# Two transformer blocks on one core: the seven-product block scheme of the first gated MLP begins one pair of loads later, with token sums read from PSUM and gate rows kept there

## Chip, cores, metric

One core of one Trainium2 chip. Times are device microseconds of one execution. The kernel before was timed in three runs.

## What is computed

Two blocks of a transformer, 512 tokens, width 1024. Each is a mixer (projections, attention or pooling, output projection), a norm with the residual, and a gated MLP with its norm. The change is inside the first block's MLP:

```python
h = rms_norm(x, ln_pre_ffn[l])
f = (jax.nn.silu(h @ w_gate[l]) * (h @ w_up[l])) @ w_down[l]
x = x + rms_norm(f, ln_post_ffn[l])
```

`w_gate` and `w_up` are 1024 x 2816, `w_down` is 2816 x 1024. All is float32.

## The kernel before

**Numbers in two parts.** Each operand of a product is split in a high part and the rest: ScalarE writes `hi` (a copy rounded to the TensorE format), VectorE (in the mixers also GpSimd) writes `lo` = raw - hi. TensorE forms hi x hi, hi x lo and lo x hi: three products for each one wanted (`products`, L1951 to L1957, whose three lines are L1954 to L1956).

**Gate and up.** `h`, turned so that features lie on partitions, is in `h_hi` and `h_lo` (8 feature groups x 512 tokens). The weights come in loads of 256 columns, gate and up in turn, 11 pairs, into the two slots of `w_raw`. A load is split by quarters (`split_hi` L1073, `split_lo` L1455).

The first pair is *straight* (`up_products` L2204): each load gives two outputs of 128 columns, in PSUM banks 0 to 3. It is formed in halves of 256 tokens, since the second half of the tokens still comes out of the norm meanwhile. A method `pair` for further straight pairs, with products of 512 tokens, is there; only the second layer runs it (ten pairs).

The other ten pairs are 20 *blocks*, `N_BLOCK = N_UP - 2` (L647), one for each load. A block is a 2 x 2 arrangement (128 columns x half of the features, half of the features x 256 tokens), formed with seven half-size products instead of eight. It needs:

- sums of its weights: GpSimd, `block_sums` L980, four operations of 128x512 into `w_sum`, written to S1, S2, S4, S3;
- sums of the tokens, once for all blocks: `t_sums`, four of 128x1024, split into `t_hi`, `t_lo` (the fourth over the free parts of `h_hi`, `h_lo`). VectorE makes sums 1, 2 and 4 (L1750 to L1769, L1738), GpSimd sum 3 (`third_turned_sum` L1008), each from high and low parts;
- the seven weight pieces S1, A11, A12, S4, S2, S3, A22, each split by ScalarE (`hi` L1262, line L1263) and VectorE (`lo` L1728, line L1730).

A *part* (L2245) is one such half-size product: 4 feature groups x 3, so 12 instructions of 256 tokens. It waits until its piece's low part is done. Blocks are interleaved (`block_period` L2255): S2 of this block, S1 and A11 of the next, S3 of this one, A12 and S4 of the next, A22 of this one. The accumulators are banks 4, 5, 6 for even blocks (gate) and 0, 1, 2 for odd ones (up): `acc(name, e)` L675. Two parts wait for sums that VectorE forms out of the accumulators (`sum_done`).

**Gate times up.** VectorE forms three sums for each block out of an accumulator and a copy that ScalarE made (`p1`, `p35`, `p5`), in lines L1788, L1808 and L1826, and reads the fourth quarter straight from bank A. For a gate block the sums go to `act_gate` in SBUF, and ScalarE applies SiLU there in place (L1333, L1344, and L1354 from PSUM). For an up block they go to `hid`, which is then multiplied by `act_gate` (L1833 for one row of 512 tokens, L1840 and L1845 for the halves of the other).

**What sets the order.** Each engine runs a program written out by hand, in order, with semaphores between: `begin` (L1271 ScalarE, L1750 VectorE) for the first blocks, `period` (L1312, L1785) for each block after that. SyncE issues the loads (`blocks` L780), each when its slot's pieces are split.

**Around it.** Ahead stands the norm: VectorE scales a token tile (`h_tok`, L1494), TensorE turns it (L1966) into PSUM (tiles 2 and 3 into banks 4 to 7), ScalarE copies the high part and VectorE the low part (L1499). Behind stand the down projection (`row_products` L2176, lines L2168 to L2172), token tile t into banks 2t and 2t+1. In its first load the last two parts of the last block (`last_p7`, `last_p4`) are put between the tiles.

## Time and profile before

| | us |
|---|---|
| median of three runs | 1368.21 (1367.76 to 1371.12) |
| profiled execution, its own time | 1370.78 |
| its span, first to last instruction | 1369.0 |
| TensorE busy in it | 1310.7 (96%) |
| VectorE | 819.0 (60%) |
| ScalarE | 665.8 (49%) |
| GpSimd | 487.0 (36%) |
| mean granted TensorE clock | 0.99 |

Times in the trace count from the first instruction. The MLP's gate and up products run from 236.8 to 485; the blocks begin at 266.65. An engine is busy while it works on an instruction; matmuls overlap, so the rate is read from the distance between starts, not from the length of one. In brackets behind a row stands how long the engine was idle before it and which line ended that.

### The profile page before, as it was taken

The numbers are of one execution on the slowest core, as the hardware profiler recorded it, in microseconds if no ns is written. First come the engines' busy times: TensorE is split into PE (matmuls) and PEld (weight loads), VectorE is DVE, ScalarE is ACT, GpSimd is POOL, SyncE is SP. The second block draws the span as 40 slices with busy tenths as digits, with TensorE's granted clock in tenths as the row PEclk, the third lists the DMA queues.
The fourth block names the chain that finished last, engine by engine and source line by source line (L and its number), as shares of the span: only waits on it lengthen the run. The fifth ranks groups of instructions, "written<-read, shape, count | busy, mean of one in ns | idle before, by whom it ended". The sixth has DMA issues, their size and how long they took to land.

```text
span 1369.0 us, 21443 instructions
## 1 busy us (share of the span) xinstructions
PE 1310.7 (96%) x7576; PEld 1167.2 (85%) x7576; DVE 819.0 (60%) x1507; ACT 665.8 (49%) x1310; POOL 487.0 (36%) x580
## 2 busy tenths in 40 slices
PE   8999989889999999999999997899999999999998
PEld 7999867889999988878999887779888888888877
DVE  4676736999999833363566665435655555533454
ACT  4666735445555522245667675524433434322352
POOL 5554682765656300046757766611000000000000
PEclk9999999999999999999999999999999999999999
DMA  6222213133233332222212322222233222222221
GB/s 185 65 66 78 63 72 113 34 121 123 92 105 109 114 102 92 85 67 73 70 47 62 71 62 77 93 96 78 93 114 99 93 92 92 92 94 96 87 92 62
DMA packets 120502, 120.52 MB, mean 88 GB/s; under 512 B 22604, under 2 KB 107291, under 8 KB 120434
## 3 DMA queue, kind: packets, MB, share of 16 engines
q1 hardware_dynamic: 118336, 112.92, 26.6%
q0 software_dynamic: 2096, 6.71, 1.5%
q8 instruction: 40, 0.66, 0.2%
q14 instruction: 28, 0.23, 0.1%
q10 hardware_dynamic: 2, 0.00, 0.0%
HBM read 117.52 MB, written 2.10 MB: 87 GB/s over the span
## 4 chain that ended last, share of the span: by engine, by line
PE 43%; DVE 4%; POOL 4%; ACT 3%; issue 2%; POOLq 0%; DVEq 0%; ACTq 0%
PE ps L1954 7%; PE ps L1956 7%; PE ps L1955 7%; PE ps L2168 4%; PE ps L2172 4%; PE ps L2170 4%; PE ps L2047 2%; PE ps L2040 2%; PE ps L2042 2%; ACT ring L1156 1%; POOL qk_rs L865 1%; POOL w_lo L903 1%; DVE ring L1579 1%; DVE prob L1622 1%; PE ps L2132 1%
## 5 line engine op out<-in xcount | busy, mean ns | idle before, releaser
L1954 PE MATMUL ps<-h_hi,w_hi 128*128 128x256 f32 (+1 forms) x784 | 259.9, 332 | 0.2 <-DVE w_lo L1459 0.2
L1956 PE MATMUL ps<-h_hi,w_lo 128*128 128x256 f32 (+1 forms) x784 | 258.4, 330 | 0.0
L1955 PE MATMUL ps<-h_lo,w_hi 128*128 128x256 f32 (+1 forms) x784 | 258.3, 329 | 0.0
L1459 DVE TENSOR_TENSOR w_lo<-w_raw,w_hi 128x512 fp32r<-128x512 f32 x220 | 140.0, 689 | 148.6 <-ACT w_hi L1082 148.6
L1082 ACT ACTIVATE w_hi<-w_raw 128x512 fp32r<-128x512 f32 x220 | 122.9, 620 | 181.6 <-PE ps L2172 163.4
L2168 PE MATMUL ps<-w_hi,st_hi 128*128 128x512 f32 x432 | 171.8, 398 | 2.7 <-DVE st_lo L1706 1.9
L2172 PE MATMUL ps<-w_hi,st_lo 128*128 128x512 f32 x432 | 171.1, 396 | 0.0
L2170 PE MATMUL ps<-w_lo,st_hi 128*128 128x512 f32 x432 | 171.1, 396 | 0.0
L2040 PE MATMUL ps<-w_hi,h_hi 128*128 128x384 f32 (+2 forms) x528 | 168.7, 329 | 2.3 <-DVE work L1561 2.0
L2042 PE MATMUL ps<-w_hi,h_lo 128*128 128x384 f32 (+2 forms) x528 | 164.8, 322 | 0.0
L1954 PEld LDWEIGHTS ps<-h_hi,w_hi 128*128 128x128 f32 x784 | 149.9, 191 | 14.2 <-DVE w_lo L1459 0.4
L1955 PEld LDWEIGHTS ps<-h_lo,w_hi 128*128 128x128 f32 x784 | 149.9, 191 | 13.1
L1956 PEld LDWEIGHTS ps<-h_hi,w_lo 128*128 128x128 f32 x784 | 149.7, 191 | 13.3
L864 POOL TENSOR_SCALAR x_ss<-x_ss 128x1 f32<-128x1 f32 x20 | 10.6, 531 | 394.8 <-ACT junk L1102 394.1
L903 POOL TENSOR_TENSOR w_lo<-w_raw,w_hi 128x384 fp32r<-128x384 f32 (+2 forms) x146 | 142.1, 988 | 21.6 <-ACT w_hi L1094 18.7
L2047 PE MATMUL ps<-w_lo,h_hi 128*128 128x384 f32 (+2 forms) x528 | 108.8, 325 | 5.7 <-POOL w_lo L903 4.9
L1173 ACT ACTIVATE prob<-prob,neg_max 128x512 f32<-128x512 f32 (+3 forms) x128 | 72.1, 563 | 82.5 <-DVE neg_max L1622 82.1
L2040 PEld LDWEIGHTS ps<-w_hi,h_hi 128*128 128x128 f32 x528 | 100.4, 190 | 4.1 <-DVE work L1561 2.2
L937 POOL TENSOR_TENSOR prob<-prob,rden 128x512 f32<-128x512 f32 (+1 forms) x96 | 69.1, 720 | 94.1 <-DVE rden L1682 93.7
L2042 PEld LDWEIGHTS ps<-w_hi,h_lo 128*128 128x128 f32 x528 | 100.7, 191 | 1.1
L2168 PEld LDWEIGHTS ps<-w_hi,st_hi 128*128 128x128 f32 x432 | 81.8, 189 | 21.9 <-issue 2.3
L2172 PEld LDWEIGHTS ps<-w_hi,st_lo 128*128 128x128 f32 x432 | 81.8, 189 | 19.1
(248 smaller groups left out, 2749.8 us busy)
## 6 DMA issues: line engine op xcount, KB each, us to landing
w_raw<-in_w_up_dram SPq DMA_DIRECT2D x33, 1024.0 KB, 5.1
w_raw<-in_w_down_dram SPq DMA_DIRECT2D x22, 1024.0 KB, 4.9
w_raw<-in_w_in_dram SPq DMA_DIRECT2D x72, 256.0 KB, 3.5
w_raw<-in_w_gate_dram SPq DMA_DIRECT2D x11, 1024.0 KB, 5.3
w_raw<-in_w_out_dram SPq DMA_DIRECT2D x8, 1024.0 KB, 5.0
w_raw<-in_w_in_dram SPq DMA_DIRECT2D x32, 128.0 KB, 2.7
w_raw<-in_w_ple_gate_dram SPq DMA_DIRECT2D x4, 1024.0 KB, 5.1
x<-in_x_dram SPq DMA_DIRECT2D x4, 512.0 KB, 5.6
```

What stands on the lines that cost most here:

```text
L903: pool.tensor_tensor(w_lo[:, c % 2, q], w_raw[:, c % 2, q], w_hi[:, c % 2, q].bitcast(F32), ALU.subtract)\
L1082: act.activation(w_hi[:, slot, q], w_raw[:, slot, q], ACT.Copy).then_inc(hi_done, 1)
L1459: dve.tensor_tensor(w_lo[:, slot, q], w_raw[:, slot, q], w_hi[:, slot, q].bitcast(F32), ALU.subtract).then_inc(lo_done, 1)
L1954: pe.matmul(out_, s_hi, m_hi, start=first and n == 0, stop=False, skip_group_check=True)
L1955: pe.matmul(out_, s_hi, m_lo, start=False, stop=False, skip_group_check=True)
L1956: mm = pe.matmul(out_, s_lo, m_hi, start=False, stop=last and n == len(pairs) - 1, skip_group_check=True)
L2040: pe.matmul(bank, h_hi[:, kb0 + i, tok], hi[:, i, :], start=half == 0 and i == 0, stop=False, skip_group_check=True)
L2042: pe.matmul(bank, h_lo[:, kb0 + i, tok], hi[:, i, :], start=False, stop=False, skip_group_check=True)
L2047: mm = pe.matmul(bank, h_hi[:, kb0 + i, tok], lo[:, i, :], start=False, stop=half == 1 and i == KH - 1, skip_group_check=True)
L2168: pe.matmul(bank, rows_hi[:, k, tok], hi[:, k, col], start=first and k == 0, stop=False, skip_group_check=True)
L2170: pe.matmul(bank, rows_hi[:, k, tok], lo[:, k, col], start=False, stop=False, skip_group_check=True)
L2172: mm = pe.matmul(bank, rows_lo[:, k, tok], hi[:, k, col], start=False, stop=last and k == RB - 1, skip_group_check=True)
```

## The change

- Straight pairs are now two. `up_products` runs `pair(1)` after the halves, and `N_BLOCK` is 18. The chunk numbers behind it move by two, so each slot keeps its parity. ScalarE and VectorE split the two additional loads in `begin`, VectorE multiplies two more rows (`first_pairs`), and the loads of the blocks start at column 512.
- Token sums: all four on VectorE (`token_sum`), GpSimd's is gone. Where the second half of the tokens is wanted, it is read from the turned tiles that still lie unsplit in banks 4 to 7 (`unsplit`), so a sum is one or two operations instead of two or three.
- For even blocks the sums of the gate go to bank 7 (`gate_row`, 512 tokens) and to half of bank 3 (`late_gate`); SiLU works there in place and the multiplications read it there. The last quarter (`early_gate`) stays in SBUF.
- The down projection begins with tile 2, then 3, 1, 0, with a wait for the last reading of bank 7 before tile 3 and of bank 3 before tile 1 (`late_gate_read`).

```diff
-        N_BLOCK = N_UP - 2
+        N_BLOCK = N_UP - 4
...
+        gate_row = ps[:, 7, :]
+        late_gate = ps[:, 3, TOK2]
+        early_gate = act_gate[:, 1, TOK1]
+        def unsplit(half):
+            return ps[:, 4 + half:8:2, :].rearrange("p t (k n) -> p t k n", n=P)
...
                 for e, w in enumerate((gate, up)):
-                    sp.wait_ge(lo_done, 4 * (C_UP1 + e + 1))
-                    sp.dma_start(by_cols((C_UP1 + e) % 2)[0], cols(w, CW)).then_inc(raw_block[e], 16)
+                    sp.wait_ge(lo_done, 4 * (C_UP1 + e + 3))
+                    sp.dma_start(by_cols((C_UP1 + e) % 2)[0], cols(w, 2 * CW)).then_inc(raw_block[e], 16)
...
             block_sums(0, 0, first=True)
-            third_turned_sum()
             block_sums(1, 1, first=True)
...
 ScalarE, begin:
+                    for m in range(2):
+                        act.wait_ge(products_done, G_UP1 + m + 1)
+                        act.activation(act_gate[:, m, :], ps[:, m, :], ACT.Silu).then_inc(gate_silu, 1)
+                    for q in range(4):
+                        split_hi(C_UP1 + 2, C_UP1 % 2, q, G_UP1 + 2)
                     act.wait_ge(t_sum, 1)
                     turned_hi(1)
+                    for q in range(4):
+                        split_hi(C_UP1 + 3, (C_UP1 + 1) % 2, q, G_UP1 + 4)
+                    act.wait_ge(t_sum, 2)
+                    turned_hi(2)
+                    act.wait_ge(t_sum, 3)
+                    turned_hi(3)
+                    for m in range(2):
+                        act.wait_ge(products_done, G_UP1 + m + 5)
+                        act.wait_ge(hid_done, m + 1)
+                        act.activation(act_gate[:, m, :], ps[:, m, :], ACT.Silu).then_inc(gate_silu, 1)
...
-                        act.activation(act_gate[:, 0, :], act_gate[:, 0, :], ACT.Silu).then_inc(gate_silu, 1)
+                        act.activation(gate_row, gate_row, ACT.Silu).then_inc(gate_silu, 1)
...
-                        act.activation(act_gate[:, 1, TOK2], act_gate[:, 1, TOK2], ACT.Silu)
+                        act.activation(late_gate, late_gate, ACT.Silu)
...
 VectorE, begin:
+                    token_sum(1)
+                    for q in range(4):
+                        split_lo(C_UP1 + 2, C_UP1 % 2, q)
+                    token_sum(2)
+                    first_pairs(0, 0)
+                    first_pairs(0, 1)
+                    token_sum(3)
+                    for q in range(4):
+                        split_lo(C_UP1 + 3, (C_UP1 + 1) % 2, q)
+                    for n in range(3):
+                        turned_lo(n + 1)
+                    token_sum(4)
                     for n, name in enumerate(("S1", "A11", "A12", "S4")):
                         lo(name, 0, n + 1)
+                    first_pairs(1, 0)
+                    first_pairs(1, 1)
                     lo("A22", 0, 5)
                     lo("S2", 0, 6)
+                    lo("S1", 1, 7)
                     dve.wait_ge(part_done, 3)
                     dve.wait_ge(part_copied, copies_made(0, 2))
-                    dve.tensor_tensor(act_gate[:, 0, TOK1], p1[:, 0, :], acc("C", 0), ALU.add).then_inc(sum_done, 1)
+                    dve.tensor_tensor(gate_row[:, TOK1], p1[:, 0, :], acc("C", 0), ALU.add).then_inc(sum_done, 1)
                     lo("A11", 1, 8)
                     lo("S3", 0, 9)
                     lo("A12", 1, 10)
                     lo("S4", 1, 11)
                     lo("A22", 1, 12)
...
+                def token_sum(n):
+                    dst = by_tiles(t_sums[n - 1][:, :, :])
+                    if n == 2:
+                        dve.wait_ge(t_sum, 1)
+                        dve.tensor_tensor(dst, unsplit(1), by_tiles(t_sums[0][:, :, :]), ALU.subtract).then_inc(t_sum, 1)
+                        return
+                    if n == 4:
+                        dve.wait_ge(t_sum, 2)
+                        hi, lo = (tokens_of(h, 1, TOK1).bitcast(F32) for h in (h_hi, h_lo))
+                        link(dve.tensor_tensor(t_sums[3][:, :, :], hi, t_sums[1][:, :, :], ALU.subtract))
+                        dve.tensor_tensor(t_sums[3][:, :, :], t_sums[3][:, :, :], lo, ALU.add).then_inc(t_sum, 1)
+                        return
+                    hi, lo = (tokens_of(h, 0, (TOK1, TOK2)[n // 2]).bitcast(F32) for h in (h_hi, h_lo))
+                    link(dve.tensor_tensor(dst, unsplit(n // 2), by_tiles(hi), ALU.subtract))
+                    dve.tensor_tensor(t_sums[n - 1][:, :, :], t_sums[n - 1][:, :, :], lo, ALU.subtract).then_inc(t_sum, 1)
+                def first_pairs(i, m):
+                    dve.wait_ge(gate_silu, 2 * i + m + 1)
+                    dve.wait_ge(products_done, G_UP1 + 4 * i + m + 3)
+                    dve.tensor_tensor(hid[:, 2 * i + m, :], act_gate[:, m, :], ps[:, 2 + m, :], ALU.mult).then_inc(hid_done, 1)
...
 VectorE, period:
-                    dve.tensor_tensor(row, row, act_gate[:, 0, :], ALU.mult).then_inc(hid_done, 1)
+                    dve.tensor_tensor(row, row, gate_row, ALU.mult).then_inc(hid_done, 1)
...
-                    dve.tensor_tensor(row, row, act_gate[:, 1, TOK2], ALU.mult)
+                    return dve.tensor_tensor(row, row, late_gate, ALU.mult)
...
 TensorE:
                 if b == 1:
+                    pair(1)
                     return
...
-            row_products(N_DOWN, C_DOWN1, N_OUT, 2, order=(3, 2, 1, 0), bank_waits={2: [(gate_silu, MT)], 0: [(hid_done, MT)]},
-                         between={2: last_p7, 1: last_p4})
+            row_products(N_DOWN, C_DOWN1, N_OUT, 2, order=(2, 3, 1, 0),
+                         bank_waits={2: [(gate_silu, MT)], 3: [(hid_done, MT - 1)], 1: [(late_gate_read, 1)],
+                                     0: [(hid_done, MT)]}, between={3: last_p7, 1: last_p4})
```

## Rows read from the trace of the kernel before

**Rows 1.** Stretches: busy us of PE, PEld, DVE, ACT, POOL; clock; DMA; GB/s.
```profile
264.00:294.00 30.00, 21.30 (x140) 20.80 (x139) 28.47 (x31) 13.98 (x27) 17.61 (x11) 0.83 0.33 106
294.00:334.00 40.00, 40.00 (x337) 39.94 (x336) 36.16 (x46) 22.96 (x46) 22.68 (x16) 1.00 0.33 106
```

**Rows 2.** Waits of TensorE, 264 to 293.4: total us, times, longest.
```profile
PE ps L1954 <- DVE w_lo L1730: 4.5, 2, 2.5
PE ps L1954 <- DVE act_gate L1788: 4.2, 1, 4.2
```

**Rows 3.** Timeline of TensorE (start, us, instruction): ends of the stretch.
```profile
263.87 0.28 PE L1956 MATMUL ps<-h_hi,w_lo 128*128 128x256 f32 x1
...
476.49 0.39 PE L2168 MATMUL ps<-w_hi,st_hi 128*128 128x512 f32 x1
```

**Rows 4.** Timeline of TensorE, steady blocks.
```profile
293.40 0.28 PE L1954 MATMUL ps<-t_hi,w_hi 128*128 128x256 f32 x1
...
303.42 0.28 PE L1954 MATMUL ps<-t_hi,w_hi 128*128 128x256 f32 x1
...
387.05 0.38 PE L1954 MATMUL ps<-h_hi,w_hi 128*128 128x256 f32 x1
...
465.05 0.28 PE L1954 MATMUL ps<-t_hi,w_hi 128*128 128x256 f32 x1
```

**Rows 5.** TensorE, second layer: groups of 955 to 1250, timeline rows.
```profile
L1954 PE MATMUL ps<-h_hi,w_hi 128*128 128x512 f32 x320 | 124.5, 389 | 0.0
...
963.18 0.40 PE L1954 MATMUL ps<-h_hi,w_hi 128*128 128x512 f32 x1
...
1180.81 0.40 PE L2168 MATMUL ps<-w_hi,st_hi 128*128 128x512 f32 x1
```

**Rows 6.** Timeline of ScalarE: a SiLU at the start and the last one.
```profile
255.54 0.60 ACT L1273 ACTIVATE act_gate<-ps 128x512 f32<-128x512 f32 x1 [3.43 <-PE ps L1956]
...
475.26 0.38 ACT L1354 ACTIVATE act_gate<-ps 128x256 f32<-128x256 f32 x1 [0.54 <-PE ps L1956]
```

**Rows 7.** Timeline of VectorE at the start, then its steady low pieces grouped.
```profile
244.59 1.27 DVE L1494 SCALAR_TENSOR_TENSOR h_tok<-x,x_rs,gain_pre 128x1024 f32<-128x1024 f32 x1
246.32 2.28 DVE L1494 SCALAR_TENSOR_TENSOR h_tok<-x,x_rs,gain_pre 128x1024 f32<-128x1024 f32 x1 [0.46 <-POOL x_rs L865]
...
253.49 3.31 DVE L1755 TENSOR_TENSOR t_sum<-t_sum,h_lo 128x1024 f32<-128x1024 f32 x1
...
264.68 1.22 DVE L1736 TENSOR_TENSOR t_lo<-t_sum,t_hi 128x1024 fp32r<-128x1024 f32 x1
265.82 0.68 DVE L1730 TENSOR_TENSOR w_lo<-w_sum,w_hi 128x512 fp32r<-128x512 f32 x1
...
281.34 2.52 DVE L1730 TENSOR_TENSOR w_lo<-w_sum,w_hi 128x512 fp32r<-128x512 f32 x1
...
L1730 DVE TENSOR_TENSOR w_lo<-w_sum,w_hi 128x512 fp32r<-128x512 f32 x71 | 68.0, 967 | 7.7 <-ACT w_hi L1263 7.5
```

**Rows 8.** Timeline of GpSimd: two weight sums.
```profile
246.26 1.26 POOL L993 TENSOR_TENSOR w_sum<-w_raw 128x512 f32<-128x512 f32 x1
...
390.29 1.63 POOL L1003 TENSOR_TENSOR w_sum<-w_raw,w_sum 128x512 f32<-128x512 f32 x1
```

**Rows 9.** DMA issues of 225 to 300: KB each, median us to landing.
```profile
w_raw<-in_w_gate_dram SPq DMA_DIRECT2D x3, 1024.0 KB, 5.2
```

**Rows 10.** Timeline of VectorE in steady blocks: sums and gated products.
```profile
386.50 0.41 DVE L1845 TENSOR_TENSOR hid<-ps,act_gate 128x256 f32 x1
...
390.68 0.41 DVE L1826 TENSOR_TENSOR act_gate<-ps,p 128x256 f32<-128x256 f32 x1
...
399.56 1.78 DVE L1833 TENSOR_TENSOR hid<-hid,act_gate 128x512 f32 x1
...
403.13 1.40 DVE L1840 TENSOR_TENSOR hid<-hid,act_gate 128x256 f32 x1
```

**Rows 11.** Timeline of TensorE: the last token tile of the norm.
```profile
248.66 1.09 PE L1966 MATMUL ps<-ident,h_tok 128*128 128x128 f32 x8 [1.65 <-DVE h_tok L1494]
```

More of the change, by code:

```diff
@@ L619, in two_blocks_kernel @@
         part_copied = sem("part_copied")
+        late_gate_read = sem("late_gate_read")
         t_sum = sem("t_sum")
-        t3_sum = sem("t3_sum")
         t_hi_done = sem("t_hi_done")
@@ L681, in raw_blocks, with by_tiles @@
             return 8 * j + (16 - 8 * e)
+        gate_row = ps[:, 7, :]
[3 more added lines that the diff above has]
+            return ps[:, 4 + half:8:2, :].rearrange("p t (k n) -> p t k n", n=P)
+        def by_tiles(rows):
+            return rows.rearrange("p k (t n) -> p t k n", n=P)
         def hid_row(n, tok):
@@ L780, in blocks @@
             def blocks(gate, up):
+                for i in range(2):
+                    for e, w in enumerate((gate, up)):
+                        load(C_UP1 + 2 * i + e, (C_UP1 + e) % 2, cols(w, CW * i))
                 for e, w in enumerate((gate, up)):
-                    load(C_UP1 + e, (C_UP1 + e) % 2, cols(w, 0))
-                for e, w in enumerate((gate, up)):
-                    sp.wait_ge(lo_done, 4 * (C_UP1 + e + 1))
-                    sp.dma_start(by_cols((C_UP1 + e) % 2)[0], cols(w, CW)).then_inc(raw_block[e], 16)
+                    sp.wait_ge(lo_done, 4 * (C_UP1 + e + 3))
+                    sp.dma_start(by_cols((C_UP1 + e) % 2)[0], cols(w, 2 * CW)).then_inc(raw_block[e], 16)
                 with sp.Fori(1, N_BLOCK // 2) as i:
@@ L1284, in begin @@
                     hi("S4", 0)
-                    act.wait_ge(t_sum, 2)
-                    turned_hi(2)
-                    act.wait_ge(products_done, G_UP1 + 4)
+                    act.wait_ge(products_done, G_UP1 + 8)
                     hi("A22", 0)
                     hi("S2", 0)
+                    act.wait_ge(t_sum, 4)
+                    turned_hi(4)
                     act.wait_ge(part_done, 1)
@@ L1353, in period @@
                     if e == 0:
-                        act.activation(act_gate[:, 1, TOK1], acc("A", e), ACT.Silu).then_inc(gate_silu, 1)
+                        act.activation(early_gate, acc("A", e), ACT.Silu).then_inc(gate_silu, 1)
                     if not last:
@@ L1736, in turned_lo @@
                     dve.tensor_tensor(low, t_sums[n - 1][:, :, :], hi.bitcast(F32), ALU.subtract).then_inc(t_lo_done, 1)
-                def difference(n, half, tok, other):
-                    dst = t_sums[n - 1][:, :, :]
-                    link(dve.tensor_tensor(dst, tokens_of(h_hi, half, tok).bitcast(F32), t_sums[other - 1][:, :, :],
-                                           ALU.subtract))
-                    dve.tensor_tensor(dst, dst, tokens_of(h_lo, half, tok).bitcast(F32), ALU.add).then_inc(t_sum, 1)
@@ L1745, in first_pair @@
-                def first_pair(m):
-                    dve.wait_ge(gate_silu, m + 1)
-                    dve.wait_ge(products_done, G_UP1 + m + 3)
-                    dve.tensor_tensor(hid[:, m, :], act_gate[:, m, :], ps[:, 2 + m, :], ALU.mult).then_inc(hid_done, 1)
+                def token_sum(n):
[13 more added lines that the diff above has]
+                    dve.tensor_tensor(t_sums[n - 1][:, :, :], t_sums[n - 1][:, :, :], lo, ALU.subtract).then_inc(t_sum, 1)
@@ L1755, in begin @@
-                    link(dve.tensor_tensor(t1, t1, tokens_of(h_lo, 0, TOK2).bitcast(F32), ALU.add))
-                    dve.tensor_tensor(t1, t1, tokens_of(h_lo, 0, TOK1).bitcast(F32), ALU.subtract).then_inc(t_sum, 1)
-                    dve.wait_ge(t_sum, 1)
-                    difference(2, 1, TOK2, 1)
-                    turned_lo(1)
+                    token_sum(1)
+                    for q in range(4):
+                        split_lo(C_UP1 + 2, C_UP1 % 2, q)
+                    token_sum(2)
@@ L1781, in sums_to @@
                 def sums_to(p, e, m, tok):
-                    return act_gate[:, m, tok] if e == 0 else hid_row(p + (m + 1), tok)
+                    return (late_gate if m else gate_row[:, tok]) if e == 0 else hid_row(p + (m + 3), tok)
                 def period(p, e, last=False, low_turned=None):
@@ L1856, in block_swiglu @@
                 dve.wait_ge(part_copied, copies_made(p, 3))
-                dve.tensor_tensor(hid_row(p + 1, TOK2), acc("A", 1), p35[:, 1, :], ALU.add).then_inc(sum_done, 1)
+                dve.tensor_tensor(hid_row(p + 3, TOK2), acc("A", 1), p35[:, 1, :], ALU.add).then_inc(sum_done, 1)
                 gated(p)
                 dve.wait_ge(part_done, parts_done(p, 2))
-                dve.tensor_tensor(hid_row(p + 2, TOK2), acc("A", 1), p5[:, 1, :], ALU.add).then_inc(sum_done, 1)
-                late_gated(p)
+                dve.tensor_tensor(hid_row(p + 4, TOK2), acc("A", 1), p5[:, 1, :], ALU.add).then_inc(sum_done, 1)
+                late_gated(p).then_inc(late_gate_read, 1)
                 dve.wait_ge(part_done, parts_done(p, 3))
-                dve.tensor_tensor(hid_row(p + 2, TOK1), acc("A", 1), act_gate[:, 1, TOK1], ALU.mult).then_inc(hid_done, 1)
+                dve.tensor_tensor(hid_row(p + 4, TOK1), acc("A", 1), early_gate, ALU.mult).then_inc(hid_done, 1)
             def conv_swiglu(c0, g0, st0):
```

50 lines of the change are left out of this document (12 added, 38 removed).

## Prediction

> **What bounds the kernel now.** I read the busy time by stage first. In the steady part of the gate and up products TensorE has no idle time. In the first 30 us of the block products it is busy for 21.3, at a mean granted clock of 0.83 [rows 1]. The waits of that stretch name the cause: 4.5 us for low weight pieces (`w_lo` L1730) and 4.2 us for one sum (`act_gate` L1788), all from VectorE [rows 2], which is itself busy for 28.5 of the 30 us [rows 1]. So the stage is bound by TensorE, except at its start, where VectorE's queue decides.
>
> The size of it: the last product of the straight pair issues at 263.87, so the next could at 263.99; the first row product of the down projection issues at 476.49 [rows 3]. Between them lie 138 parts of 12 products: 19 whole blocks of seven, and five parts. A block without a wait takes 303.42 - 293.40 = 10.02 us, so a part takes 1.431 us [rows 4]. 138 parts are 197.5 us, and the stretch is 212.5: 15.0 us are lost. From 303.42 to 465.05 lie 16 blocks in 161.63 us, against 160.3: 1.3 us, in small gaps once in two blocks, such as the one before the product at 387.05 [rows 4]. The other 13.7 are lost at the start: 8.7 as waits, about 5 at the lower clock and around the restarts [rows 1 to 3].
>
> **The change part by part.** Times below are those of before, unshifted, unless said.
>
> *One pair of loads straight, 18 blocks for 20.* A straight pair is 96 products of 512 columns. The second layer's ten such pairs, 320 products on each of three lines, take 1180.81 - 963.18 = 217.6 us, so a pair is 21.8 us [rows 5]. Two blocks are 20.0. The new stretch is 21.8 + 124 x 1.431 = 199.2 us, against 212.5. If nothing at all is lost, 13.3 us are saved. The arithmetic alone costs 1.8; the rest is what the straight pair covers. What the start loses afterwards must be taken off.
>
> *Does the straight pair start without a wait?* It needs its gate chunk split. ScalarE does the second SiLU after the second gate product, about 258.5 (the first began at 255.54 [rows 6]), then four quarters of the same 512 elements as that SiLU, 0.60 each [rows 6]: 261.5. VectorE takes 0.68 a quarter when alone [rows 7] and follows to about 262.2, before 264.0. On VectorE this split stands behind token sum 1, which is now two operations where it was three, and none of the slow ones at 3.31 us [rows 7], since GpSimd has nothing to do then. Alone, 1024 elements take 1.2 us [rows 7]: it ends at about 254.5. The up chunk is needed 48 products later, at 274.9. VectorE gets there after token sum 2, two `hid` rows and token sum 3, at 267.3; alone its quarters end at 270.0, and with one weight sum of GpSimd (1.26 us [rows 8]) before each of them at 275.1. I take 273.7 and no wait, with 0.2 us as the bad end.
>
> *Are the first blocks ready at 285.8?* GpSimd's weight sums wait for a load now issued behind the gate chunk's low split at 262.2, landing 5.2 us later [rows 9], and run from 267.5 to about 275. ScalarE's high pieces of block 0 follow at 275.5 to 278. VectorE: up chunk to 273.7, then GpSimd's last sum to 275, three low token sums and token sum 4 (five operations of 1.2) to 281, and four pieces, one sum of GpSimd among them, to 285. The first is there at 281.7, four us before its part, and each of the others too. The token operations that stood between the pieces before are gone or done.
>
> *The wait that is added.* `first_pairs(1, 1)` stands on VectorE before pieces A22, S2 and S1 of the next block, and waits for the last product of the straight pair, at 285.8. Behind it are queued a `hid` row, eight low pieces and two sums, wanted one by one: the fifth part at 291.5, the eighth (S3, with its sum) at 295.8. Counted to that sum: 0.68 + 8 pieces + 2 x 0.41 [rows 7, 10]. At 0.68 a piece that is 6.9 us; at the steady mean of 0.967 [rows 7] it is 9.2; there are 10.0. So it fits with little room. I take 0.8 us for the start, and keep 0 and 9.0 (below) as ends.
>
> *The weight sums leave the stretch 246 to 267.* The first of them began at 246.26 [rows 8], and the scaling of the last token tile beside it took 2.28 us [rows 7] where its neighbour of the same size took 1.27 [rows 7]. TensorE waited 1.65 us for it at 248.66 [rows 11]. Without the sum it ends 1.0 earlier. ScalarE's and VectorE's copies of the tile (1.0 and 1.2) then still end before TensorE's next 24 products do, so 1.0 us is saved. The low end is 0, if another wait ends last there.
>
> *Gate rows in two PSUM banks.* Per two blocks, three sums write PSUM, two SiLU go PSUM to PSUM, and two multiplications read one operand there. The multiplications took 1.78 and 1.40 us because both inputs lay in SBUF and GpSimd was at work [rows 10]. A sum with one input from PSUM took 0.41 at 390.68 although GpSimd's sum ran from 390.29 to 391.92 [rows 8, 10]. So I expect 0.7 and 0.4, some 2.1 us of VectorE per pair. That by itself is off the path. But the gap before 387.05 ends just after the multiplication of L1845 (386.50 to 386.91 [rows 10]), which stands behind them in the queue; 0.7 us earlier removes it. Of 8 pairs x 0.16 = 1.3 us I leave 0.4. No row shows a write to PSUM by either engine here. From the nearest rows, sums of 0.41 and SiLU of 0.60, its cost lies between -0.1 and +0.3 us an operation. The five on VectorE then add 1.5 us a pair at most, less than the 2.1 it gets back.
>
> The Trainium skill (SBUF — State Buffer, Who interferes with whom) says that VectorE with two SBUF inputs and GpSimd exclude each other while they read, and that with one SBUF input it does not. By that rule the two multiplications lose their stretch entirely, and the trace agrees (1.78 against 0.41). Against the change speaks the table in VectorE: DVE Perf Modes, The TRN2 errata, which gives an operation from PSUM 62 cycles more than one from SBUF; by it, as an estimate, 65 ns are added to each of five operations a pair, 3 us of VectorE time in all, and the sum would stay, as VectorE does not bound there. The trace does not agree: its SBUF rows of 512 and 1024 elements, 0.68 and 1.22, put 256 elements at 0.41, and the row with a PSUM input has 0.41.
>
> *The end of the stage.* The down projection now begins with tile 2, whose bank is read by the last SiLU. That ran 475.26 to 475.64, and the row product came at 476.49 [rows 3, 6]: 0.85 us to spare. Tile 3 waits for a multiplication of bank 7 that has a row tile and a part, 4.2 us, to get done; `late_gate_read` has longer. Nothing.
>
> **The sum.** 13.3 + 1.0 - 0.8 - 0.4 = 13.1, rounded down to 13.0 us. The profiled execution took 1370.78 us with a span of 1369.0, so its like would take 1357.8. It was 2.6 above the median of 1368.21, from which I take the forecast: **1355.2 us**.
>
> **The rivals.**
> 1. *The queue behind the held `hid` row is late.* It takes the place of the waits removed. If the eight pieces take 1.78 us each, as the multiplication of the same size did beside GpSimd [rows 10], VectorE needs 15.7 us for 10.0: TensorE waits 5.7, and a wait like that costs some 3.3 in clock afterwards (5 were lost around 8.7). 13.3 + 1.0 - 9.0 - 0.4 gives 4.9: 1363.3. For it: such durations are frequent at the start before. Against: each needs a GpSimd sum at its side, and only four to six fall in these 10 us. The mild half, 1 to 5 us lost, is likelier than the full price.
> 2. *Only the straight pair does anything:* reads of PSUM don't free VectorE and the token tile wins nothing. The gaps stay at 1.3 and the 1.0 is not had: 13.3 - 0.8 - 1.3 = 11.2, so 1357.0. The 0.41 beside a running GpSimd speaks against it.
> 3. *Slower.* The same place as rival 1, at the price of the longest piece of the old start, 2.5 us (281.34 [rows 7]): 8 x 2.52 + 1.5 = 21.7, TensorE waits 11.7, and with the clock 15.0. Then 13.3 + 1.0 - 15.0 - 0.4 = -1.1: 1369.3. It decides from 13.9 us lost, a piece mean of about 2.4. It goes over 0.3% slower when the up chunk of the straight pair is late by 3 us too: 1372.5. GpSimd has about eight sums of 1.3 us in the whole start, too few for that.
>
> **How the numbers follow.** Forecast 0.66 (1353.5 to 1358 by itself, with the run to run spread of 1367.8 to 1371.1 in mind), rival 1 0.18, mostly below 1361, rival 2 0.07, rival 3 0.09 with its neighbours, of which 0.04 is slower by over 0.3% and 0.05 no difference. A measurement of this kernel can tell 0.3%, 4.1 us, from no change. The range reaches to the middle of rival 1: 1353.2 to 1361.0. Faster 0.91, within 0.3% 0.05, slower 0.04.
>
> **What would show it.** Right: between the two straight pairs TensorE does not idle; the second takes 21.8 us; the block products begin with waits under 1 us in sum, and the granted clock stays at 1.00 from 236 on; `hid` multiplications take 0.7 and 0.4; the wait for the last token tile shrinks to about 0.65; the first row product of the down projection comes 13 us sooner. Wrong: TensorE waits for `w_lo` L1730 or for a sum in `ps` after the second pair, and the clock falls there; or a part of each block waits for `sum_done`, 18 times over. The forecast falls above all if VectorE, after its hold, is not back in step by the eighth part.

## The result and the profile after

Six runs of the changed kernel have a median of 1357.88 us (1357.60 to 1358.93), six of the kernel before 1369.80 (1367.76 to 1372.36). The ratio is 0.9914, with a 95% interval of 0.9901 to 0.9926: 11.9 us faster. The forecast was 1355.2, with a range to 1361.0. Its base of 1368.21, the median of three runs, turned out 1.6 below that of six, and its gain of 13.0 is 1.1 more than was had.

| | before | after |
|---|---|---|
| span of the profiled execution | 1369.0 | 1356.3 |
| TensorE busy | 1310.7 | 1305.6 |
| VectorE | 819.0 | 799.5 |
| ScalarE | 665.8 | 659.8 |
| GpSimd | 487.0 | 465.3 |

First the stretches, which answer to [rows 1]. The columns are the same.

```profile
236.00:264.00 28.00, 27.15 (x214) 26.12 (x213) 20.42 (x23) 14.98 (x23) 8.13 (x10) 1.00 0.24 75
264.00:286.00 22.00, 22.00 (x103) 18.35 (x102) 20.39 (x19) 7.47 (x12) 8.39 (x5) 1.00 0.30 96
286.00:296.00 10.00, 10.00 (x83) 9.88 (x82) 7.70 (x10) 7.32 (x14) 5.72 (x6) 1.00 0.34 107
296.00:306.00 10.00, 7.40 (x61) 7.03 (x60) 10.00 (x11) 4.66 (x11) 7.63 (x5) 1.00 0.66 210
306.00:346.00 40.00, 40.00 (x338) 40.00 (x337) 37.36 (x47) 22.96 (x47) 23.78 (x17) 1.00 0.34 106
```

TensorE is busy without a gap from 264 to 296, where before it had 21.30 of 30 us. It loses 2.6 us between 296 and 306, and there VectorE is busy for 10.00 of 10. The granted clock is 1.00 (2.4 GHz) in every row; in [rows 1] it was 0.83. The waits of TensorE from 230 to 312 (total, times, longest), for [rows 2]:

```profile
PE ps L1984 <- DVE h_tok L1503: 1.8, 2, 1.1
PE ps L1972 <- DVE ps L1806: 1.4, 1, 1.4
PE ps L1972 <- issue: 1.2, 1, 1.2
PE ps L1972 <- DVE w_lo L1468: 0.2, 1, 0.2
```

Of the first row, 0.66 us is the wait for the last token tile (1.65 in [rows 11]). Where 4.5 us of low pieces and 4.2 us of a sum stood, there is one wait of 1.4 us for a sum, and one of 1.2 for which the view names no engine. The timeline of TensorE gives their places and the marks used below; it answers to [rows 3, 4, 11]:

```profile
238.69 0.28 PE L1972 MATMUL ps<-h_hi,w_hi 128*128 128x256 f32 x1
...
249.54 1.09 PE L1984 MATMUL ps<-ident,h_tok 128*128 128x128 f32 x8 [0.66 <-DVE h_tok L1503]
...
264.87 0.40 PE L1972 MATMUL ps<-h_hi,w_hi 128*128 128x512 f32 x1
...
286.65 0.28 PE L1972 MATMUL ps<-t_hi,w_hi 128*128 128x256 f32 x1
...
298.22 0.39 PE L1972 MATMUL ps<-t_hi,w_hi 128*128 128x256 f32 x1 [1.37 <-DVE ps L1806]
...
303.99 0.36 PE L1972 MATMUL ps<-h_hi,w_hi 128*128 128x256 f32 x1 [1.23 <-issue]
...
305.49 0.28 PE L1972 MATMUL ps<-t_hi,w_hi 128*128 128x256 f32 x1
...
455.79 0.28 PE L1972 MATMUL ps<-t_hi,w_hi 128*128 128x256 f32 x1
...
467.24 0.39 PE L2186 MATMUL ps<-w_hi,st_hi 128*128 128x512 f32 x1
```

The second straight pair runs from 264.87 to 286.65, 21.78 us, with no wait before it. The blocks then run to the first row product at 467.24. Their 124 parts at 1.431 would take 177.5 us and took 180.59, so 3.1 are lost. All of it is lost at the start: from 305.49 to 455.79 lie 15 blocks in 150.30 us, 10.02 each.

The timeline of VectorE shows why, and what came before:

```profile
248.20 1.29 DVE L1503 SCALAR_TENSOR_TENSOR h_tok<-x,x_rs,gain_pre 128x1024 f32<-128x1024 f32 x1 [0.47 <-POOL x_rs L877]
...
260.45 2.50 DVE L1468 TENSOR_TENSOR w_lo<-w_raw,w_hi 128x512 fp32r<-128x512 f32 x4 [4.98 <-ACT w_hi L1084]
...
268.13 4.69 DVE L1468 TENSOR_TENSOR w_lo<-w_raw,w_hi 128x512 fp32r<-128x512 f32 x4
...
280.73 0.69 DVE L1739 TENSOR_TENSOR w_lo<-w_sum,w_hi 128x512 fp32r<-128x512 f32 x1
...
286.92 0.69 DVE L1767 TENSOR_TENSOR hid<-act_gate,ps 128x512 f32<-128x512 f32 x1 [2.01 <-PE ps L1974]
...
289.77 0.97 DVE L1739 TENSOR_TENSOR w_lo<-w_sum,w_hi 128x512 fp32r<-128x512 f32 x1 [0.96 <-ACT w_hi L1265]
291.17 0.43 DVE L1792 TENSOR_TENSOR ps<-p,ps 128x256 f32<-128x256 f32 x1 [0.42 <-PE ps L1974]
...
293.60 1.76 DVE L1739 TENSOR_TENSOR w_lo<-w_sum,w_hi 128x512 fp32r<-128x512 f32 x1
295.29 2.53 DVE L1739 TENSOR_TENSOR w_lo<-w_raw,w_hi 128x512 fp32r<-128x512 f32 x1
297.74 0.42 DVE L1806 TENSOR_TENSOR ps<-ps,p 128x256 f32<-128x256 f32 x1
...
302.68 1.21 DVE L1745 TENSOR_TENSOR h_lo<-t_sum,h_hi 128x1024 fp32r<-128x1024 f32 x1
```

The straight chunks are split in time: the gate chunk by 262.95 for 264.87, the up chunk by 272.82 for a product some 11 us after 264.87. The first piece of a block is there at 281.4. Then the `hid` row of the straight pair holds VectorE until 286.92. From there to the end of the sum in L1806, at 298.16, it takes 11.2 us: two waits of 0.96 and 0.42, and two pieces of 1.76 and 2.53. TensorE goes on 0.06 us after that sum. The second wait ends at 303.99, 0.10 us after the operation of L1745, which is `turned_lo(4)`, the low part of the fourth token sum. So the "issue" of the waits view is a wait for VectorE too; the kernel below in which `turned_lo(4)` stands earlier has no such wait.

**Marks.** In what follows, *stretch* is the time from the first gate product (238.69 here) to the first row product of the down projection (467.24): 228.55 us. Before, it ran from 236.83 to 476.49 [rows 3]: 239.66. The difference is 11.1. The trace's own clock shows the row product only 9.25 us sooner, since this execution reached its first gate product 1.86 later.

### The profile page after: what moved, and what is told of

It is laid out like the page before. It is cut to its first block, busy times and chain, and to the rows that moved or that the text cites. A ratio compares the mean times of both kernels' runs of the same rounds, so it can differ in the third digit from the quotient of the medians.

```text
span 1356.3 us, 21161 instructions
## 1 busy us (share of the span) xinstructions
PE 1305.6 (96%) x7504; PEld 1159.7 (86%) x7504; DVE 799.5 (59%) x1494; ACT 659.8 (49%) x1297; POOL 465.3 (34%) x569
## 4 chain that ended last, share of the span: by engine, by line
PE 43%; DVE 4%; POOL 4%; ACT 3%; issue 2%; POOLq 0%; DVEq 0%; ACTq 0%
PE ps L1972 7%; PE ps L1973 7%; PE ps L1974 7%; PE ps L2186 4%; PE ps L2188 4%; PE ps L2190 4%; PE ps L2058 2%; PE ps L2065 2%; PE ps L2060 2%; ACT ring L1158 1%; POOL qk_rs L877 1%; POOL w_lo L915 1%; DVE ring L1588 1%; DVE prob L1631 1%; PE ps L2150 1%
## 5 line engine op out<-in xcount | busy, mean ns | idle before, releaser
L1468 DVE TENSOR_TENSOR w_lo<-w_raw,w_hi 128x512 fp32r<-128x512 f32 x228 | 147.1, 698 | 155.2 <-ACT w_hi L1084 155.2
L1084 ACT ACTIVATE w_hi<-w_raw 128x512 fp32r<-128x512 f32 x228 | 127.3, 621 | 185.1 <-PE ps L2190 164.7
```

The source lines that it names most:

```text
L1084: act.activation(w_hi[:, slot, q], w_raw[:, slot, q], ACT.Copy).then_inc(hi_done, 1)
L1468: dve.tensor_tensor(w_lo[:, slot, q], w_raw[:, slot, q], w_hi[:, slot, q].bitcast(F32), ALU.subtract).then_inc(lo_done, 1)
```

## The experiments

Each was profiled once; those with an interval were also timed against the kernel before, whose medians beside them were 1368.43 to 1370.02. The last column is the time of the blocks, from their first part to the first row product.

| kernel | us | ratio to before | stretch | blocks |
|---|---|---|---|---|
| before | 1369.80 | | 239.66 | 209.84 |
| the kernel before, again | 1370.21 (one) | | 239.45 | 209.61 |
| after | 1357.88 | 0.9914 (0.9901 to 0.9926) | 228.55 | 180.59 |
| after, again | 1358.89 | 0.9921 (0.9905 to 0.9938) | 228.54 | 180.59 |
| after, token sums as before | 1357.10 | 0.9911 (0.9895 to 0.9928) | 229.41 | 180.57 |
| after, gate rows in SBUF | 1361.25 | 0.9942 (0.9925 to 0.9958) | 229.90 | 181.96 |
| after, straight pair alone | 1360.04 (one) | | 230.76 | 181.94 |
| before, gate rows in PSUM | 1368.03 | 0.9991 (0.9981 to 1.0001) | 238.38 | 208.55 |
| after, GpSimd beside the last tile | 1359.50 (one) | | 229.53 | 180.57 |
| after, other order at the start | 1357.53 | 0.9917 (0.9901 to 0.9933) | 227.38 | 179.44 |
| other order at the start, second form | 1357.64 | 0.9915 (0.9900 to 0.9931) | 227.40 | 179.45 |
| after, small weight sums | 1356.86 (one) | | 226.85 | 178.89 |
| blocks at once | 1362.19 | 0.9951 (0.9936 to 0.9965) | 230.61 | 203.46 |

**The yardstick: both kernels again.** No edit in either.

> The changed kernel a second time, for a second trace. From the first product of the gate and up stage to the first row product of the down projection the first trace took 228.6 us (before: 239.7). If that stretch is what the change moved and the rest of the span is execution to execution variation, it is 228.6 within 0.3 again, while the parts outside it may move by one or two us. If the 1.9 us that the stage began later belongs to the change, it begins at 238.7 again, against 236.8 before.

> The kernel before a second time, for a second trace. If the start of the stage and the time after it vary between executions of one kernel, its first gate product comes at another time than 236.8 by a us or more, or the span behind the first row product of the down projection differs from 892.5 by one to three us; the stretch between them stays at 239.7 within 0.3. If the change moved them, both stay as they were.

The stretch came out at 228.54 and 239.45, within 0.01 and 0.21 of the first profiles. The change is worth 11.0 us in it (10.9 and 11.1); the 11.9 of the medians, with its interval of 10.1 to 13.6, holds that. The rest of the program does not repeat so well: the first gate product comes between 236.6 and 239.2 in these profiles, and the time from the first row product to the second layer's first 512-column product lies between 483.1 and 486.7, in either kernel. The later begin in the first profile of the changed kernel is not the change's doing either, as the second profile of the kernel before has it at 239.06. So terms of about 1 us are read from the stretch and not from medians.

**Token sums as before, all else of the change kept.**

```diff
+                    if n == 1:
+                        t1 = t_sums[0][:, :, :]
+                        link(dve.tensor_tensor(t1, tokens_of(h_hi, 0, TOK2).bitcast(F32), tokens_of(h_hi, 0, TOK1).bitcast(F32), ALU.subtract))
+                        link(dve.tensor_tensor(t1, t1, tokens_of(h_lo, 0, TOK2).bitcast(F32), ALU.add))
+                        dve.tensor_tensor(t1, t1, tokens_of(h_lo, 0, TOK1).bitcast(F32), ALU.subtract).then_inc(t_sum, 1)
+                        return
...
+            third_turned_sum()
```

> The changed kernel with the token sums formed as before: three operations for the first on VectorE, two for the second, the third on GpSimd directly after the norm, all from high and low parts in SBUF. Theory (the straight pair makes the room, the PSUM reads only add to it): VectorE loses 1.2 + 3 x 2.1 us beside GpSimd before the gate chunk's low split, which then ends about 264 to 265 and delays the second straight pair by 0 to 1.5 us; the up chunk and the blocks aren't later, since VectorE has slack of 2 us before 286.8; start losses stay at 3.1. Sum: 0 to 2 us slower than the changed kernel, 1358 to 1360. Rival (without the PSUM reads the start is as late as before): TensorE waits 5 us or more between the two pairs or at the first block, 1363 or more.

The timeline of VectorE in this kernel, at token sum 1 and the split of the gate chunk:

```profile
254.71 3.31 DVE L1762 TENSOR_TENSOR t_sum<-t_sum,h_lo 128x1024 f32<-128x1024 f32 x1
258.05 3.32 DVE L1763 TENSOR_TENSOR t_sum<-t_sum,h_lo 128x1024 f32<-128x1024 f32 x1
261.29 4.71 DVE L1475 TENSOR_TENSOR w_lo<-w_raw,w_hi 128x512 fp32r<-128x512 f32 x4
```

With GpSimd's third sum back at their side, the operations take 3.31 again, as in [rows 7], and the gate chunk is split only by 266.00. The second straight pair waits 0.57 us for it, and the blocks start 0.88 us later in the stretch. From there on nothing differs (180.57 against 180.59). So reading the turned tiles from PSUM and taking the third sum from GpSimd, which were not tried one by one, are together worth 0.86 us, by letting the straight pair start in time. The medians do not resolve it: this kernel's, 1357.10, lies 0.8 and 1.8 below the two of the changed kernel, where it was expected up to 2 above.

**Gate rows in SBUF, all else of the change kept.**

```diff
-        gate_row = ps[:, 7, :]
-        late_gate = ps[:, 3, TOK2]
+        gate_row = act_gate[:, 0, :]
+        late_gate = act_gate[:, 1, TOK2]
...
                     dve.wait_ge(part_copied, copies_made(0, 2))
+                    dve.wait_ge(hid_done, 3)
```

The added wait keeps the first sum from overwriting the straight pair's gate row before it is read.

> The changed kernel with the gate rows in SBUF as before (gate_row and late_gate in act_gate), all else as changed. Theory: the gated multiplications take 1.78 and 1.40 us again instead of 0.7 and 0.4, and the gaps of 0.1 to 0.2 us before every second block's first h product return: 15 blocks of the steady part take 1.0 to 1.3 us more than 150.3. The start loses as much or up to 0.5 more. So 1 to 1.8 us slower than the changed kernel, about 1359.3. Rival (the gaps have another cause, such as the order of the start): the steady part stays at 150.3 and the time within 0.5 us of the changed kernel's.

**Only the gate rows in PSUM, in the kernel before** (the same lines the other way round, and the tile order 2, 3, 1, 0).

> The kernel before with the gate rows in PSUM alone (and the tile order of the down projection that this needs); 20 blocks, old start. Theory: the 16 steady blocks take 160.3 us instead of 161.6, the start loses its 13.7 us as before or up to 1 less, so 1.3 to 2.3 us faster than before, about 0.1%. Rival (VectorE's slack in the steady part also shortens the start by several us): 4 us or more faster.

The first gives 1.35 us in the stretch, the second 1.1 to 1.3 (239.45 and 239.66 less 238.38). In both, the waits at the start are unchanged, so the term comes from the steady blocks: with the rows in SBUF the 15 blocks take 151.67 us (305.04 to 456.71) for 150.30. The 1.37 us answer to the small gaps once in two blocks [rows 4], and with the rows in PSUM none of it is left. The median of the kernel with the rows in SBUF is 3.4 and 2.4 us above the two of the changed kernel, 1 to 2 more than the stretch gives. What that comes from stays open: three of its four executions have a mean granted clock of 0.992, all ten of the changed kernel 0.994 or 0.995. What VectorE does meanwhile, grouped by line over 140 us of steady blocks (seven pairs; busy us, mean ns, then idle before). With the rows in SBUF:

```profile
L1739 DVE TENSOR_TENSOR w_lo<-w_sum,w_hi 128x512 fp32r<-128x512 f32 x56 | 55.0, 992 | 4.8 <-ACT w_hi L1265 4.8
L1739 DVE TENSOR_TENSOR w_lo<-w_raw,w_hi 128x512 fp32r<-128x512 f32 x42 | 45.6, 1085 | 4.7 <-ACT w_hi L1265 4.7
L1852 DVE TENSOR_TENSOR hid<-hid,act_gate 128x512 f32 (+1 forms) x7 | 12.4, 1778 | 0.0
L1859 DVE TENSOR_TENSOR hid<-hid,act_gate 128x256 f32 (+1 forms) x7 | 9.8, 1406 | 0.0
```

and in the changed kernel:

```profile
L1739 DVE TENSOR_TENSOR w_lo<-w_sum,w_hi 128x512 fp32r<-128x512 f32 x57 | 61.9, 1086 | 11.4 <-ACT w_hi L1265 11.0
L1739 DVE TENSOR_TENSOR w_lo<-w_raw,w_hi 128x512 fp32r<-128x512 f32 x42 | 49.6, 1182 | 1.1 <-ACT w_hi L1265 1.1
L1851 DVE TENSOR_TENSOR hid<-hid,ps 128x512 f32 (+1 forms) x7 | 4.7, 675 | 0.0
L1844 DVE TENSOR_TENSOR ps<-ps,p 128x256 f32<-128x256 f32 x7 | 2.9, 420 | 0.0
...
L1858 DVE TENSOR_TENSOR hid<-hid,ps 128x256 f32 (+1 forms) x7 | 2.9, 408 | 0.0
```

The two multiplications fall from 1.78 and 1.41 us to 0.68 and 0.41: 2.1 us a pair of blocks, as forecast. But the pieces grow from a mean of 1.03 us (100.6 us over 98) to 1.13 (111.5 over 99). 14 of them a pair take 1.4 us of the 2.1 back. The pieces have both inputs in SBUF, as the multiplications had, and they now meet the GpSimd sums that the multiplications met before. Among the pieces that start in these 140 us, one with no GpSimd sum beside it takes 0.68 us in either kernel. With one beside it, it takes 1.38 in the mean with the rows in SBUF and 1.45 with the rows in PSUM, and the number of such pieces goes from 48 of 97 to 56 of 98. VectorE's time falls by 0.7 us a pair only. The gap goes since the multiplications stand ahead of the last bank's reader in the queue: with the rows in SBUF it (L1864) ends at 338.12, just before TensorE's late product at 338.26, and with them in PSUM (L1863) at 337.37.

**GpSimd beside the last token tile.** One GpSimd operation of 128x512 with two SBUF inputs is put back where the first weight sum used to run.

```diff
             norm(1, True)
+            pool.wait_ge(gain_in[1], 16)
+            pool.wait_ge(gain_in[2], 16)
+            link(pool.tensor_tensor(w_sum[3].rearrange("p k n -> p (k n)"), gain_pre[:, 0:512], gain_post[:, 0:512], ALU.add))
             block_sums(0, 0, first=True)
```

> The changed kernel with one additional GpSimd sum of 128x512 from two SBUF operands (its result unused), put where GpSimd's first weight sum stood before, directly behind the norm's last power. Theory: VectorE's scaling of the last token tile takes 2.3 us again instead of 1.29, TensorE waits 1.65 instead of 0.66 for it, and the stretch from the first gate product to the end of the first straight pair is 27.2 us again instead of 26.2. Rival (the tile was late for another reason): the scaling stays at 1.3 and the stretch at 26.2.

```profile
248.25 2.28 DVE L1506 SCALAR_TENSOR_TENSOR h_tok<-x,x_rs,gain_pre 128x1024 f32<-128x1024 f32 x1 [0.46 <-POOL x_rs L877]
```

GpSimd's operation started at 248.18 and took 1.26 us. The scaling beside it is back at 2.28 us (1.29 without), TensorE's wait for it at 1.65 (0.66), and the stretch is 0.98 longer, all of it before the second straight pair. This term was forecast to the tenth, and without GpSimd's operation no other wait takes the place of the one that goes.

**The straight pair alone:** both edits above that undo the PSUM parts, in one kernel.

> The kernel before with the second straight pair alone: token sums in the old way (the third on GpSimd behind the norm) and the gate rows in SBUF. If the three parts add up as the single undoings say (token sums from PSUM 0.9 us, gate rows 1.4), the stretch from the first gate product to the first row product is 228.5 + 0.9 + 1.4 = 230.8 us, 8.8 less than before's 239.6, so the pair and the weight sums' later place bring four fifths of the gain. Rival (parts cover for each other): 232 or more.

The stretch is 230.76. The two parts add: 228.55 + 0.86 + 1.35 = 230.76. So of 239.56 (the mean of the two profiles of before) the pair takes 8.8, with the 1.0 of the token tile in it, the token sums 0.9 and the gate rows 1.35. These shares hold in this order, the pair first; the last experiment takes them in the other.

**Another order at the start.** `turned_lo(4)` goes ahead of S1 of the next block, and the sum that TensorE waited for goes ahead of A22.

```diff
                     lo("S2", 0, 6)
+                    turned_lo(4)
                     lo("S1", 1, 7)
...
                     lo("S4", 1, 11)
+                    first_sum(0, 0)
                     lo("A22", 1, 12)
...
-                    if low_turned:
-                        turned_lo(low_turned)
```

> The changed kernel with two operations of VectorE's start moved ahead: the low part of the fourth token sum directly after piece S2 of block 0 (into a gap in which VectorE waits for ScalarE), and the first sum into bank 7's second half before the low piece A22 of block 1. Theory: the 3.1 us that the start still loses are these two arrivals, 1.4 for the sum and 1.2 to 1.5 for the fourth token sum's low part; both go, and the first steady block comes 2 to 3 us sooner: 2.5 us faster than the changed kernel, 1355.4. Rival (VectorE has too much to do there in any order): another operation comes late by the same amount, and the time moves by less than 1 us.

Its waits of TensorE from 237 to 470:

```profile
PE ps L1976 <- DVE ps L1848: 0.8, 1, 0.8
...
PE ps L1976 <- DVE ps L1808: 0.4, 1, 0.4
```

and what VectorE did in front of them:

```profile
289.14 2.28 DVE L1745 TENSOR_TENSOR h_lo<-t_sum,h_hi 128x1024 fp32r<-128x1024 f32 x1 [0.18 <-ACT h_hi L1268]
291.34 1.78 DVE L1739 TENSOR_TENSOR w_lo<-w_sum,w_hi 128x512 fp32r<-128x512 f32 x1
```

The stretch is 1.2 us shorter where 2.5 were expected and the rival had less than 1. In its new place `turned_lo(4)` meets a sum of GpSimd and takes 2.28 us for 1.21, and the piece behind it takes 1.78 for 0.97. The work fills the hole that ScalarE left and is stretched there. A second form moved the sum ahead of S4 too, and the sums of the second row (`second_rows`) ahead of a piece:

```diff
+                    if summed:
+                        second_rows(p, e)
...
-                    second_rows(p, e)
+                    if not summed:
+                        second_rows(p, e)
```

> As the first reordering of the start (fourth token sum's low part after piece S2 of block 0), with the first half-row sum of block 0 before piece S4 of block 1 rather than before A22, and the third sum before piece A11 instead of behind it. Theory: TensorE's two waits that were left, 0.35 and 0.83 us, each stood behind one low piece that GpSimd stretched to 1.8; both go and the stretch from the first gate product to the first row product is 226.2 us (changed kernel 228.5, first reordering 227.4). Rival (VectorE's work up to there is the bound): the waits move to the next piece, 227.0 or more.

```profile
PE ps L1979 <- DVE hid L1808: 1.6, 1, 1.6
```

Both waits are gone, and one of 1.62 us has come at 308.94, for the first sum of the next block. The stretch is the same, 227.40, where 226.2 was expected. The rival was right for this step: an order gives back 1.2 of the 3.1 us, and the second form only moves what is left to another wait.

**Small weight sums.** GpSimd's sums of the first two blocks work on 8 columns in place of 128. Four memsets by GpSimd, placed ahead of them, leave the rest at zero, so what the first two blocks give is not what the MLP asks for.

```diff
-                s1, s2, s3, s4 = (s[:, :, :] for s in w_sum)
-                a11, a21, a12, a22 = (block_of(name, e) for name in ("A11", "A21", "A12", "A22"))
+                wide = 8 if first else P
+                s1, s2, s3, s4 = (s[:, :, 0:wide] for s in w_sum)
+                a11, a21, a12, a22 = (block_of(name, e)[:, :, 0:wide] for name in ("A11", "A21", "A12", "A22"))
...
+            for s in w_sum:
+                link(pool.memset(s[:, :, :], 0.0))
```

> The changed kernel with GpSimd's weight sums of blocks 0 and 1 over 8 of the 128 columns (four operations of 128x32 in place of 128x512 each); the rest of those sums is left at zero, so the first two blocks' products are not those of the reference. Theory: VectorE's low pieces at the start lose their stretch (1.76 and 2.53 us to 0.7), so the start loses 0 to 1 us where the changed kernel loses 3.1. Rival (the queue is too long whatever GpSimd does): it still loses 2 us or more.

```profile
291.92 0.69 DVE L1742 TENSOR_TENSOR w_lo<-w_sum,w_hi 128x512 fp32r<-128x512 f32 x1 [0.21 <-ACT w_hi L1268]
292.53 0.69 DVE L1742 TENSOR_TENSOR w_lo<-w_raw,w_hi 128x512 fp32r<-128x512 f32 x1
```

These are the two pieces that took 1.76 and 2.53 us in the changed kernel. The wait for the sum is gone; only the one before `turned_lo(4)` is left, 1.15 us. The blocks take 178.89 and lose 1.4 us in place of 3.1, between the 0 to 1 of the theory and the 2 or more of the rival. So 1.7 of the 3.1 are the meeting of VectorE and GpSimd, and the other 1.4 the wait for `turned_lo(4)` and its restart.

**Blocks at once.** Can the PSUM sums do without the second straight pair? Twenty blocks as before, with the token sums and gate rows of the change and an order for VectorE to match:

```diff
-        N_BLOCK = N_UP - 4
+        N_BLOCK = N_UP - 2
...
                     token_sum(1)
                     token_sum(2)
+                    turned_lo(1)
                     token_sum(3)
...
+                    first_pair(0)
+                    turned_lo(2)
+                    first_pair(1)
                     lo("A22", 0, 5)
                     lo("S2", 0, 6)
+                    token_sum(4)
                     lo("S1", 1, 7)
+                    turned_lo(3)
```

> 20 blocks as before, no second straight pair, but the token sums read from PSUM (all on VectorE), the gate rows in PSUM, the low part of token sums 2 to 4 and the sums put where each is wanted. Asked: is it the straight pair that removes the 13.7 us of the start, or would the rest alone do it, which would also save the pair's 1.8 us of arithmetic? Theory 1 (VectorE has room enough once the token sums are short): by addition VectorE has S1 to S4 of block 0 split at 262, two us before TensorE wants them, and the start then loses 1 to 4 us: stretch 26.2 + 1 to 4 + 198.9 = 226 to 229 us, the time 1355.5 to 1358.5. Rival (the cover of 21.8 us is needed): TensorE waits at the first part or within the first two blocks for 6 us or more, the stretch is 232 or more.

Its waits of TensorE:

```profile
PE ps L1988 <- DVE h_tok L1505: 1.6, 1, 1.6
PE ps L1976 <- DVE hid L1805: 1.6, 1, 1.6
PE ps L1976 <- DVE w_lo L1741: 1.5, 3, 0.7
PE ps L1976 <- DVE ps L1848: 1.5, 1, 1.5
```

The first part starts without a wait, 27.15 us after the first gate product, where it took 29.82 before. But VectorE is then busy for 29.96 of the 30 us from 264 to 294, and the blocks lose 203.46 - 197.5 = 6.0 us. The stretch is 230.61, 2.1 longer than with the pair. Neither expectation came true: the theory had 226 to 229 with 1 to 4 us lost, the rival 232 or more. Of the 11.0 us of the change, 8.95 can be had without the pair, by the token sums, the gate rows and the new order of VectorE's queue together; what each of the three brings here was not tried. The pair alone brought 8.8. The two do not add, as each removes most of the same loss at the start. The pair costs 1.8 us of arithmetic, and brings 1.0 at the token tile, which here still stands beside GpSimd's weight sum, and 2.9 at the start (6.0 against 3.1): 2.1 net. The medians put this kernel 3.3 to 4.3 us behind the changed one, and the stretch accounts for 2.1 of that; the rest is not explained.

No version here beats the changed kernel by more than a median can show.

## Why the prediction came out as it did

The forecast's times are on the clock of the trace before; in the trace after, the stage begins 1.86 later and the first straight pair, with the last token tile in it, is 1.0 shorter.

- *The straight pair and 18 blocks for 20, 13.3 us before losses:* right. The pair took 21.78 us (21.8), and a block 10.02.
- *No idle before the second pair:* right, 1.9 us to spare for the gate chunk and, at the up chunk, about 3. By the kernel with the token sums as before, that cover hangs on them: 0.57 us of wait otherwise.
- *First blocks ready:* right. The first piece was there at 281.4 for a part at 286.65, 5.2 us ahead where four were forecast.
- *The last token tile, 1.0:* right, 0.98 by itself.
- *The start, 0.8 us:* this step failed, though the time came out within the range. It lost 3.1, with 2.60 us of waits where under 1 was forecast. The count to the eighth part had 9.2 us for 10.0, and 11.2 were needed. Two things were mis-sized. The mean of 0.967 for a piece is that of the whole kernel, and here eight pieces took 8.95 us, 1.12 each: four took 0.68 or 0.69, two some 0.96, and two, beside GpSimd's sums, 1.76 and 2.53. And the count had VectorE never waiting, but ScalarE, just released by the same last product, wrote the high part of the fourth token sum (1.05 us) and a copy of an accumulator (0.36) ahead of S1's and left VectorE idle for 0.96 us; 0.42 more went by until the third part was done. Beyond that, the step left one instruction out: `turned_lo(4)`, which stands in `period(0, 0, low_turned=4)` and not in `begin`. It cost 1.23 us of wait. "Three low token sums" had been counted where the code has four. The sign that the forecast named for its own fall, VectorE not back in step by the eighth part, came true; the loss was small enough to leave the total in the range.
- *Gate rows in PSUM, 0.9 of the 1.3 us of gaps:* mis-sized the other way. All 1.3 went; 0.4 had been held back. The durations 0.7 and 0.4 were right (0.68 and 0.41), and a write to PSUM costs nothing to speak of (0.42 against 0.41), within the range given. That the pieces would take 1.4 of the 2.1 us back was not seen.
- *The end of the stage, nothing:* right. TensorE has no wait from 440 to 480.
- *The sum:* 13.3 + 1.0 - 3.1 - 0 = 11.2, against 11.0 in the stretch. The forecast's 13.1, rounded down to 13.0, became 11.2 by 2.3 more at the start and 0.4 less in the gaps. So the two errors of the sum partly cancelled, and the base, 1.6 too low, added to what was left.
- *The rivals:* the first, a late queue behind the held row, happened in its mild half (1 to 5 us lost), at 3.1. Its full price did not come, since only two of eight pieces took 1.76 us or more, and since the clock did not fall. The second (reads from PSUM free nothing) gave almost the right size, 11.2, for the wrong reason: both of its parts were had, 1.0 and 1.35. The third didn't occur. Its sum took the 3.3 us for the clock that belong to a wait of 5.7; at the same rate, 5 lost around 8.7, its wait of 11.7 would have cost 6.7.
- *The clock:* right at 1.00 from 236 on. In the kernel before, 8.7 us of waits cost about 5 more at a clock of 0.83 and around restarts. Here 2.6 us of waits cost 0.5 more.

Two rules of the Trainium skill were weighed in the forecast. With the first (the Trainium skill, SBUF — State Buffer, Who interferes with whom) the runs agree: the same multiplication beside GpSimd's sums takes 1.78 us with both inputs in SBUF and 0.68 with one in PSUM. The forecast did not apply it to the pieces, which have two SBUF inputs as well and went from 1.03 to 1.13. The second (the Trainium skill, VectorE: DVE Perf Modes, The TRN2 errata), the extra time of a PSUM source, is not seen here. In the changed kernel 128x512 with a PSUM input takes 0.67 to 0.69 us, and a piece with both inputs in SBUF and no GpSimd sum beside it 0.68. The forecast's estimate also charged it to five operations a pair, where three of them, the sums, read an accumulator in PSUM before the change too.

## To carry to other kernels

When a change holds an engine's queue at one instruction, count all that stands behind it by reading both the engine's own program and that of the engine which feeds it after the same release, and look for operations passed in as an argument. Take the duration of a contended operation from the stretch that has the same neighbours, not from a mean over the kernel. A bank that frees one engine's operation from contention moves the contention to the next operation of the same kind, so credit the gap that it closes and not the busy time that it seems to save. And where two changes remove the same loss, the share of each depends on which is counted first.

## What the hardware showed beside this

- SiLU from PSUM to PSUM is no slower than from PSUM to SBUF. Timeline of ScalarE in the changed kernel, the first of them; in [rows 6] the same size into SBUF took 0.60.

```profile
298.62 0.59 ACT L1342 ACTIVATE ps<-ps 128x512 f32<-128x512 f32 x1
```

- Waits of 1.37 and 1.23 us, 5.8 us apart, left the granted clock at 1.00 (2.4 GHz). So did five waits of 0.41 to 1.62 us, ended between 273.73 and 291.56, in the kernel with the blocks at once. In the kernel before, the clock stood at 0.50 (1.2 GHz) after the wait of 2.50 us that ended at 266.65 and after the one of 4.23 that ended at 284.85, and at 1.00 around the one of 1.97 that ended at 277.53. The second profile of that kernel shows the same. Whether it is the length of the wait that decides is not shown. Three stretches of the kernel before, columns as in [rows 1]:

```profile
268.00:270.00 2.00, 2.00 (x11) 2.00 (x10) 2.00 (x3) 0.81 (x2) 0.24 (x1) 0.50 0.00 0
276.00:278.00 2.00, 0.47 (x4) 0.51 (x5) 2.00 (x5) 1.14 (x3) 0.83 (x1) 1.00 0.27 91
286.00:288.00 2.00, 2.00 (x11) 2.00 (x10) 1.87 (x2) 0.19 (x1) 1.92 (x2) 0.50 0.91 313
```

- With GpSimd's 128x1024 sums at their side, two of VectorE's of that size and both inputs in SBUF take 3.31 and 3.32 us, against 1.22 alone.
